# Order of SyncE's transfers in two SwiGLU stages, and the weight sums of the down product moved from GpSimd to VectorE

## The reference

```
mod = silu(c) W_ada + b_ada            -> shift, scale, gate for 3 sub-layers
x  += 1/2 (1+g0) * SwiGLU_1(mod0(RMSNorm(x)))      SwiGLU(h) = (silu(h W_gate) * (h W_up)) W_down
x  += (1+g1) * W_out [ RMSNorm(attention) | RMSNorm(B * conv3(C * x_c)) ]
x  += 1/2 (1+g2) * SwiGLU_2(mod2(RMSNorm(x)))
x   = RMSNorm(x) * g_final
```

## Time and profile before

| | |
|---|---|
| median of 3 runs | 2056.69 us (2052.34 to 2064.18) |
| the profiled execution's own time | 2066.67 us |
| its span (first to last instruction) | 2064.9 us |
| mean granted TensorE clock | 0.949 |
| busy: TensorE, VectorE, ScalarE, GpSimd | 1875.0, 1189.4, 681.7, 686.7 us |

### The profile page before, as it was taken

How to read it: one execution, slowest core, us unless ns; L and a number is a source line. 1 busy time by engine, 2 the same in 40 slices (tenths; PEclk the granted TensorE clock), 3 DMA queues, 4 the chain that set the end, 5 groups by cost and what they waited for, 6 DMA issues and landing times. The chain is left out here.

```text
span 2064.9 us, 21706 instructions
## 1 busy us (share of the span) xinstructions
PE 1875.0 (91%) x8448; PEld 1537.8 (74%) x8448; DVE 1189.4 (58%) x1269; ACT 681.7 (33%) x879; POOL 686.7 (33%) x380
## 2 busy tenths in 40 slices
PE   5489989998869999999999999977999999979997
PEld 5367777777757877887778878856888888867876
DVE  2975565656569656234572347778444454439656
ACT  2342222322323444322343224334333323313442
POOL 1364445544348000121121211146335344359000
PEclk9789999999989999998699999998999999989998
DMA  7024443444672632222023230111322423572633
GB/s 306 0 92 160 182 157 137 158 179 181 239 269 87 226 96 87 83 95 94 21 99 106 82 102 32 67 36 48 138 85 91 138 76 109 186 309 87 224 92 107
DMA packets 84590, 261.42 MB, mean 127 GB/s; under 512 B 8096, under 2 KB 8096, under 8 KB 82976
## 3 DMA queue, kind: packets, MB, share of 16 engines
q1 hardware_dynamic: 79904, 252.01, 35.0%
q10 hardware_dynamic: 4608, 8.39, 1.1%
HBM read 211.61 MB, written 48.76 MB: 126 GB/s over the span
## 5 line engine op out<-in xcount | busy, mean ns | idle before, releaser
L1915 PE MATMUL pair<-cb,w_hi 128*128 128x512 f32 x880 | 355.3, 404 | 75.6 <-DVE w_lo L1316 34.1
L1915 PE MATMUL pair<-h_hi,w_hi 128*128 128x512 f32 x792 | 315.5, 398 | 56.5 <-DVE h_lo L1335 25.0
L1916 PE MATMUL pair<-cb,w_hi 128*128 128x512 f32 x880 | 352.0, 400 | 0.0
L1917 PE MATMUL pair<-cb,w_lo 128*128 128x512 f32 x880 | 351.1, 399 | 0.0
L1916 PE MATMUL pair<-h_lo,w_hi 128*128 128x512 f32 x792 | 313.3, 396 | 0.0
L1917 PE MATMUL pair<-h_hi,w_lo 128*128 128x512 f32 x792 | 312.8, 395 | 0.0
L1915 PEld LDWEIGHTS pair<-cb,w_hi 128*128 128x128 f32 x880 | 171.4, 195 | 119.5 <-issue 43.6
L1915 PEld LDWEIGHTS pair<-h_hi,w_hi 128*128 128x128 f32 x792 | 152.0, 192 | 93.9 <-issue 40.2
L1917 PEld LDWEIGHTS pair<-cb,w_lo 128*128 128x128 f32 x880 | 171.1, 194 | 37.1
L1916 PEld LDWEIGHTS pair<-cb,w_hi 128*128 128x128 f32 x880 | 171.6, 195 | 35.5
L1316 DVE TENSOR_TENSOR w_lo<-s_w,w_hi 128x1024 fp32r<-128x1024 f32 x66 | 103.1, 1563 | 126.8 <-ACT w_hi L887 126.8
(11 more groups left out here) (166 smaller groups left out, 3426.6 us busy)
## 6 DMA issues: line engine op xcount, KB each, us to landing
raw<-hs SPq DMA_DIRECT2D x70, 512.0 KB, 3.6
ada_w<-w_ada SPq DMA_DIRECT2D x55, 512.0 KB, 5.3
raw<-w_mix SPq DMA_DIRECT2D x48, 512.0 KB, 3.5
hs<-tt SPq DMA_DIRECT2D x22, 1024.0 KB, 4.2
a<-w_f1o SPq DMA_DIRECT2D x30, 512.0 KB, 6.7
a<-w_f2o SPq DMA_DIRECT2D x30, 512.0 KB, 6.9
ga<-w_f1i SPq DMA_DIRECT2D x22, 512.0 KB, 6.3
ua<-w_f1i SPq DMA_DIRECT2D x22, 512.0 KB, 3.6
```

The source lines that it names most:

```text
L1915: nc.tensor.matmul(dst, lh, rh, start=first, stop=False, skip_group_check=True)
L1916: nc.tensor.matmul(dst, lh, rl, start=False, stop=False, skip_group_check=True)
L1917: return nc.tensor.matmul(dst, ll, rh, start=False, stop=False, skip_group_check=True)
```

## The change

In the groups the `ada` load of a c comes first, ua1's load is at c=2, and `hid_store(g-1)` comes after ua2's load at c=4. The semaphore count of `hs_out` is without the `g1` part of the last group, which is stored by itself (`hid_last`) with its own semaphore; `hid_load(5)` waits for that. At the switch the loads and stores are ordered anew, and x loads and a12's loads are spread between the later `hid_load`s. `down_sums` goes from GpSimd's program to VectorE's, one step of each kind per chunk.

```diff
+        def stored(F, g):
+            return (48 * NG - 16) * F + 48 * (g + 1)
...
             def hid_store(F, g):
...
-                if G:
-                    sp.wait_ge(hs_out, 48 * G)
+                if g:
+                    sp.wait_ge(hs_out, stored(F, g - 1))
...
+                if g < NG - 1:
+                    sp.dma_start(hs[4:6, :, a:a + T]..., gbuf[par][1][:]...).then_inc(hs_out, 16)
+                sp.dma_start(hs[6, :, a:a + T], gbuf[par][0][:, T:2 * T]).then_inc(hs_out, 16)
+
+            def hid_last(F):
+                sp.wait_ge(hid1_done, NG * (F + 1))
+                a = (NG - 1) * T
                 sp.dma_start(hs[4:6, :, a:a + T]...,
-                             gbuf[par][1][:]...).then_inc(hs_out, 16)
-                sp.dma_start(hs[6, :, a:a + T], gbuf[par][0][:, T:2 * T]).then_inc(hs_out, 16)
+                             gbuf[(NG - 1) % 2][1][:]...).then_inc(hs_last, 16)
...
                     for c in range(GC):
-                        if c == 1:
+                        if c in slots:
+                            t += 1
+                            ada_load(t)
+                        if c == 2:
                             sp.wait_ge(s3_sum, G + 1)
                             group_load(F, g + 1, 2, ua1, ua1_in)
-                        if c == 2:
-                            if g:
-                                hid_store(F, g - 1)
                             sp.wait_ge(w_ready, n + (5 if g else 6))
                             group_load(F, g + 1, 0, ga1, ga1_in)
...
                             group_load(F, g + 1, 3, ua2, ua2_in)
-                        if c in slots:
-                            t += 1
-                            ada_load(t)
+                            if g:
+                                hid_store(F, g - 1)
...
+                last_ada(1)
                 sp.wait_ge(s3_sum, G + 1)
-                sp.dma_start(col(raw, 0, CW), hs[STEP_HS[0], :, 0:CW]).then_inc(hraw_in[0], 16)
-                last_ada(1)
+                hid_load(F, 0)
+                last_ada(2)
                 sp.wait_ge(w_used, n + 2)
                 for c in range(4):
                     down_load(F, 0, a11, c, a11_in)
-                hid_store(F, g - 1)
-                last_ada(2)
+                last_ada(3)
...
                 sp.wait_ge(w_ready, n + 7)
-                sp.dma_start(col(raw, CW, CW), hs[STEP_HS[0], :, CW:2 * CW]).then_inc(hraw_in[1], 16)
-                last_ada(3)
+                hid_load(F, 1)
+                last_ada(4)
+                hid_store(F, g - 1)
                 sp.wait_ge(w_used, n + 4)
                 for c in range(OC):
                     down_load(F, 1, a21, c, a21_in)
-                last_ada(4)
+                hid_load(F, 2)
                 sp.wait_ge(w_used, n + 5)
                 for c in range(OC - 1):
                     down_load(F, 3, a22, c, a22_in)
-                last_ada(5)
-                hid_load(F, 2)
                 hid_load(F, 3)
-                sp.wait_ge(hs_out, 48 * G)
+                sp.wait_ge(hs_out, stored(F, g - 1))
                 hid_load(F, 4)
-                hid_store(F, g)
+                hid_last(F)
+                sp.wait_ge(hs_last, 16 * (F + 1))
+                hid_load(F, 5)
                 sp.wait_ge(w_used, n + 7)
                 down_load(F, 3, a22, OC - 1, a22_in)
-                for c in range(OC):
-                    down_load(F, 2, a12, c, a12_in)
-                sp.wait_ge(hs_out, 48 * (G + 1))
-                hid_load(F, 5)
-                if F == 0:
-                    sp.wait_ge(ada_done, ADA_TILES)
-                x_load(F, 0, 1, 0)
-                x_load(F, 1, 0, KH)
-                x_load(F, 2, 0, 0)
-                x_load(F, 3, 1, KH)
                 for m in range(6, OQ):
+                    if m == 8:
+                        hid_store(F, g)
+                        sp.wait_ge(hs_out, (48 * NG - 16) * (F + 1))
+                        if F == 0:
+                            sp.wait_ge(ada_done, ADA_TILES)
+                        x_load(F, 0, 1, 0)
+                    if m == 13:
+                        x_load(F, 1, 0, KH)
+                    if m == 18:
+                        x_load(F, 2, 0, 0)
+                    if m == 25:
+                        x_load(F, 3, 1, KH)
                     hid_load(F, m)
+                    c = m - OC - 2
+                    if 0 <= c < OC:
+                        down_load(F, 2, a12, c, a12_in)
...
-            down_sums(0)          # GpSimd's program, and down_sums(1) likewise
...
+            def down_sums(F, q):              # VectorE's program
+                c = q - 1                     # a22 = a21 + a22        (S1)
+                if 0 <= c < OC:
+                    dve.wait_ge(a21_in[c], 16 * (F + 1))
+                    dve.wait_ge(a22_in[c], 32 * F + 16)
...
+                c = q - 5                     # a22 = a22 - a11        (S2)
...
+                c = q - 10                    # a12 = a12 - a22        (S4)
+                if 0 <= c < OC:
+                    dve.wait_ge(os2_sum, OC * F + c + 1)
+                    dve.wait_ge(a12_in[c], 32 * F + 16)
...
+                c = q - 16                    # a11 = a11 - a21        (S3)
...
                     if q + 3 < OQ:
                         out_lo(F, q + 3)
                         hid_lo(F, q + 3)
+                    down_sums(F, q)
```

More of the change, by code:

```diff
@@ L255, in build @@
         hs_out = sem("hs_out")
+        hs_last = sem("hs_last")
         a11_in = [sem(f"a11_in{c}") for c in range(OC)]
@@ L455, in hid_store @@
                              tt[:].rearrange("p (b c) -> p b c", b=4)).then_inc(hs_out, 16)
+                if g < NG - 1:
+                    sp.dma_start(hs[4:6, :, a:a + T].rearrange("b p c -> p b c"),
+                                 gbuf[par][1][:].rearrange("p (b c) -> p b c", b=2)).then_inc(hs_out, 16)
+                sp.dma_start(hs[6, :, a:a + T], gbuf[par][0][:, T:2 * T]).then_inc(hs_out, 16)
+            def hid_last(F):
+                sp.wait_ge(hid1_done, NG * (F + 1))
+                a = (NG - 1) * T
                 sp.dma_start(hs[4:6, :, a:a + T].rearrange("b p c -> p b c"),
-                             gbuf[par][1][:].rearrange("p (b c) -> p b c", b=2)).then_inc(hs_out, 16)
-                sp.dma_start(hs[6, :, a:a + T], gbuf[par][0][:, T:2 * T]).then_inc(hs_out, 16)
+                             gbuf[(NG - 1) % 2][1][:].rearrange("p (b c) -> p b c", b=2)).then_inc(hs_last, 16)
             def down_load(F, q, dst, c, done):
@@ L719, in hid_blocks @@
                 if g:
-                    pool.wait_ge(hs_out, 48 * G)
+                    pool.wait_ge(hs_out, stored(F, g - 1))
                 else:
@@ L739, in groups @@
                 hid_blocks(F, NG - 1)
[L741 to L751, removed]
-                    pool.wait_ge(os2_sum, OC * F + c + 1)
-                    pool.wait_ge(a12_in[c], 32 * F + 16)
-                    nc.gpsimd.tensor_tensor(col(a12, a, w), col(a12, a, w), col(a22, a, w), ALU.subtract).then_inc(os4_sum, 1)
-                pool.wait_ge(os2_sum, OC * (F + 1))
-                for c in range(OC):
-                    a, w = 2 * T * c, out_w(c)
-                    nc.gpsimd.tensor_tensor(col(a11, a, w), col(a11, a, w), col(a21, a, w), ALU.subtract).then_inc(os3_sum, 1)
             power(0)
@@ L852, in _ @@
             groups(1)
-            down_sums(1)
             power(8)
@@ L1022, in copy_s1 @@
                 if g >= 2:
-                    act.wait_ge(hs_out, 48 * (G - 1))
+                    act.wait_ge(hs_out, stored(F, g - 2))
                 elif F:
@@ L1541, in groups @@
                 hid0(F, NG - 1, FI[F] + GC * NG)
+            def down_sums(F, q):
+                c = q - 1
+                if 0 <= c < OC:
+                    a, w = 2 * T * c, out_w(c)
+                    dve.wait_ge(a21_in[c], 16 * (F + 1))
+                    dve.wait_ge(a22_in[c], 32 * F + 16)
+                    nc.vector.tensor_tensor(col(a22, a, w), col(a21, a, w), col(a22, a, w), ALU.add).then_inc(os1_sum, 1)
+                c = q - 5
+                if 0 <= c < OC:
+                    a, w = 2 * T * c, out_w(c)
+                    dve.wait_ge(w_ready, FO[F] + OC + c + 1)
+                    nc.vector.tensor_tensor(col(a22, a, w), col(a22, a, w), col(a11, a, w), ALU.subtract).then_inc(os2_sum, 1)
+                c = q - 10
+                if 0 <= c < OC:
+                    a, w = 2 * T * c, out_w(c)
+                    dve.wait_ge(os2_sum, OC * F + c + 1)
+                    dve.wait_ge(a12_in[c], 32 * F + 16)
+                    nc.vector.tensor_tensor(col(a12, a, w), col(a12, a, w), col(a22, a, w), ALU.subtract).then_inc(os4_sum, 1)
+                c = q - 16
+                if 0 <= c < OC:
+                    a, w = 2 * T * c, out_w(c)
+                    dve.wait_ge(os2_sum, OC * F + c + 1)
```

(1 more changed line is left out.)

## The result

The changed kernel took a median of 1962.24 us (1953.43 to 1975.74, 4 runs) against 2054.52 us of the kernel before in the same session: ratio 0.9551, 95% interval 0.9481 to 0.9622. A second, independent comparison gave 1962.45 against 2055.35, 0.9552 (0.9502 to 0.9602). The forecast was 1973 with 1956 to 2000, faster.

A forecast was written before the change was run, and what follows sets the result against it. TensorE, busy 91%, was taken to lose time in waits and lower clock; gains 44.5+23.6+20.8 = 88.9 us off 2066.7 (profiled) or 2056.7 (median) gave 1977.8 or 1967.8, the middle 1973, range 1956 to 2000.

The forecast's parts named there:

- The groups: First feed-forward's groups: the whole wait for a late ada tile goes, 44.5 us gained, bounds 22 to 45.5.
- The first switch: First feed-forward's last product to chunk 14: 26.6 us lost before, 3 left after, 23.6 gained.
- the sum for the stall, 3: First switch: 3 us left after the change, 1 of stall and 2 of lower clock, bounds 0 and 8.
- The second switch: Second feed-forward, c22 to chunk 14: 21.8 us lost before, 1 left after (bounds 0 and 4), 20.8 gained.
- (a): First switch: 13.8 us stall at chunk 3 from mod operations beside GpSimd's sums; these take 6.4 us in place of 16.9.
- (b): Down products from chunk 12: w_lo and h_lo take 3.42 us each beside GpSimd for 1.22, 6.8 per 5.44 us chunk.
- B: Groups: the ada wait stays in part as a tile lands late, half of 44 stays, 1995 us; chance 0.10.
- C: Switches fill up again, stores ahead of loads that chunks 3 and 8 need; half of 48 stays, 1997 us; 0.10.
- D: Groups: the ada wait is one of transfer, not order, so only the switches gain, 2018 us; chance 0.03.
- E: Groups of both feed-forwards: the later store delays GpSimd's blocks and S1 to S3; slower, 2083 at 5.5 a group; 0.05.

The follow-up runs named there:

- experiment 1: Changed kernel with the groups' old order of ada loads, ua1 and store; 2008.06 us, ratio 0.9755 to the kernel before.
- experiment 2: Kernel before with only the groups' new order (ada loads ahead, store behind ua2's load); 2013.03 us, ratio 0.9801.
- experiment 5: Changed kernel, but in the groups only the store is moved, ua1 and ada loads ordered as before; 1973.91 us, one execution.
- experiment 6: Changed kernel, but in the groups only the ada loads are moved ahead, the store stays at c=2; 1970.49 us, one execution.
- experiment 7: Changed kernel with the whole last store issued and waited for ahead of hid_load(5) again; 1967.33 us, one execution.
- kernel 9: Changed kernel with a22's last chunk and all six a12 loads ahead of hid_load(5) again; 1968.06 us, one execution.
- experiment 4: Kernel before with only the weight sums moved to VectorE, all transfers in the old order; 2051.60 us, ratio 0.9977.
- experiment 3: Changed kernel with the down product's weight sums back on GpSimd in their old order; 1999.74 us, ratio 0.9734 to the kernel before.

## Why the prediction held, point by point

- **The groups** (44.5 forecast, measured in the forecast's own terms below). The cause was right: an `ada` tile held behind the wait for `tt`, three stores and a weight tile (experiments 1, 2, 5, 6). Between TensorE's last products of groups 1 and 10 were 386.46 us and are now 342.7 (172.37 to 515.09): 43.7, with 2.2 for the first one; 45.9 against 44.5. No stall stayed. The forecast had both moves as needed; experiments 5 and 6 show the store's to be enough and the loads' to be nearly so, which it didn't see.
- **The first switch** (23.6; measured 24.0: from 515.09 to chunk 14 at 593.80 are 78.7 us, before 102.67). The order of events was as worked out, and close: hid_load(3) landed by 533.49, t=23.5 after S3's end (said 23.6), the `mod` operations took 6.45 us (said 6.4), chunk 3 was 2.28 us late (said 1, and 2 of lower clock that did not come in this profile). That the sum for the stall, 3, came out near is partly luck: where the lower clock did come (kernels 5, 7 and 9), the same wait cost 1.4 us more.
- **The second switch** (20.8; measured 22.4 by the marks, which reach past the forecast's chunk 14). No wait stayed of the 1 us taken. But of its reasons one was wrong: "its load was issued after the whole store of the last group had been waited for" named the store as the cost. Experiment 7 puts the store back and loses nothing here; experiment 4, with the whole old order, has the stalls (7.36 and 6.69 us). So they are of several transfers together; which pair it takes stays open. hid_load(8) came later than said (t=48.6, by the cast at 558.57 in the first stage, for 44.5), with 3 us left to chunk 8 and 1.2 to chunk 9.
- **GpSimd and VectorE.** Said: 3.42 us for `w_lo` beside GpSimd, 1.22 without. In the changed kernel's switches no `w_lo` or `h_lo` takes more than 1.92. What the forecast did not see is that the edits need each other: it gave (a) and (b) to the sums and the rest to the transfers, as if they added. Experiment 3 cost 38 us where the expectation drawn from it gave 21, and experiment 4 won 9 by the marks and nothing that timing tells.
- **The total.** 92.6 by the marks against 88.9 in the sum. The forecast's 1973 is 10.8 above the median, 5 of it from taking the middle between the profiled execution and the median: the 12 us by which the profiled execution of before stood over the median lie for some 7 us in the mixer (716.5 us in that profile, 709.4 in the median of the fourteen), outside everything that the change touches; where the other 5 lie isn't known. So the median less the sum (1967.8) was the better number.
- **Rivals.** B (a late tile): no `ada_w` wait is left in the groups. C (the switch fills up): not met, but near, 1.2 us at chunk 9. D: refuted by the groups at 38.12. E: the second feed-forward's groups are at 342.7 us before and after; the later store holds nobody.

## What to carry to other kernels

A queue that runs in order makes everything behind a wait late, also what has nothing to do with it: look for the wait that a queue stands in, not only for what it moves, and put last the transfer that nobody needs soon. A wait on an engine off the critical path is worth only what exceeds its slack (8.8 us cost 4.9, 5.2 us cost 0.8), so measure where the next engine sees it. When two limits lie one behind the other, undoing or doing one edit alone says little of its worth (0 and 5 us alone, 21 together): test both ways before an edit is called useless. And before a microsecond or two at a mark are put to an edit, look for the same difference in a kernel that doesn't have the edit (experiments 5 and 7).

## What the runs showed of the hardware

The durations of VectorE beside GpSimd fit an exclusive alternation, not a shared rate. A 128x1024 `w_lo` takes 1.22 us alone; beside GpSimd's 128x512 `tt` blocks 2.30 (1.08 more), beside its 128x1024 sums 3.42 (2.2 more), and GpSimd's sums grow from 2.39 to 3.3 by about one VectorE operation. An 8-column operation waits as long as a large one, 2.26 us in place of 0.17. VectorE's x updates, with one input in PSUM, don't slow down: four in 2.71 us beside GpSimd's sums in the kernel before, four in 2.72 without. The Trainium skill (SBUF — State Buffer, "Who interferes with whom") states this rule, the blocking for a whole instruction and the exemption of an instruction with at most one SBUF input outside the two-port modes; these rows agree. The exemption doesn't reach the TENSOR_SCALAR on `mod`, which has one SBUF tensor and took 2.27 us beside the sums; whether it ran in a two-port mode no run shows.

TensorE's granted clock differs between executions of one program: the six timed runs of the changed kernel go from 1953.99 us at a mean of 0.978 to 1977.12 us at 0.962. The mixer's 697 to 719 us over the fourteen profiles, with the same code, is a scatter of that size; what sets it was not tested. In the first feed-forward of the kernel before the clock fell in the groups after some of the waits on `s`: after 4.35 us the next matmul took 0.77 us (217.20), after 4.54 us 0.47 (429.84). In the changed kernel, from 140 to 900 us, it stayed at its upper level (2.4 GHz):

```profile
140.00:900.00 760.00, 746.36 (x3360) 615.30 (x3358) 476.95 (x501) 259.97 (x295) 229.88 (x121) 1.00 0.49 166
```
```profile
140.00:560.00 420.00, 388.30 (x1658) 317.61 (x1656) 246.78 (x224) 120.84 (x121) 200.66 (x79) 0.97 0.46 166
```

The first row is the changed kernel, the second the kernel before in its groups (columns as in the earlier trace rows).
